# The order of rounded and remainder rows in the second block of each feed-forward pair

## The reference, cut to what matters

```
def swiglu(x, w_gate, w_up, w_down):
    return (jax.nn.silu(x @ w_gate) * (x @ w_up)) @ w_down

h = x
for i in range(DEPTH):                       # DEPTH = 2
    h = h + 0.5 * swiglu(rms_norm(h, norm_ff1[i]), ffn1_gate[i], ffn1_up[i], ffn1_down[i])
    hn = rms_norm(h, norm_mix[i])
    h = h + (hybrid mixer of hn if i is even, differential attention of hn if i is odd)
    h = h + 0.5 * swiglu(rms_norm(h, norm_ff2[i]), ffn2_gate[i], ffn2_up[i], ffn2_down[i])
return rms_norm(h, final_norm)
```

## Time and profile before

| | |
|---|---|
| median of 3 runs | 1066.17 us |
| the profiled execution's own time | 1065.55 us |
| its span in the profile | 1063.7 us |
| PE busy | 1050.4 us (99%), 6678 matmuls |
| PEld busy | 944.8 us (89%) |
| DVE busy | 792.3 us (74%) |
| ACT busy | 611.4 us (57%) |
| DMA queue of the weights | 188.89 MB, 63.0% of 16 engines |

### The profile page before, as it was taken

How to read it: one execution, slowest core, us unless ns; L and a number is a source line. 1 busy time by engine, 2 the same in 40 slices (tenths; PEclk the granted TensorE clock), 3 DMA queues, 4 the chain that set the end, 5 groups by cost and what they waited for, 6 DMA issues and landing times.

```text
span 1063.7 us, 18486 instructions
## 1 busy us (share of the span) xinstructions
PE 1050.4 (99%) x6678; PEld 944.8 (89%) x6678; DVE 792.3 (74%) x1137; ACT 611.4 (57%) x980; POOL 51.1 (5%) x70
## 2 busy tenths in 40 slices
PE   9999999999999999999999999999999999999997
PEld 8888888899998998888888888888999998888886
DVE  6788776679868878887666888776699578888653
ACT  6555554468976665555445665543456756656541
POOL 0200011100000000000111000011100000000011
PEclk9999999999998999999999999999999999999999
DMA  8866775549644656667755666685566446667671
GB/s 250 213 195 193 211 205 162 156 124 259 175 114 125 200 156 191 189 194 206 208 158 159 196 196 189 197 218 165 146 169 165 120 127 200 190 195 204 188 200 40
DMA packets 369283, 190.14 MB, mean 179 GB/s; under 512 B 5920, under 2 KB 368704, under 8 KB 369232
## 3 DMA queue, kind: packets, MB, share of 16 engines
q1 hardware_dynamic: 368976, 188.89, 63.0%
q0 software_dynamic: 256, 0.59, 0.3%
HBM read 187.86 MB, written 1.07 MB: 178 GB/s over the span
## 4 chain that ended last, share of the span: by engine, by line
PE 94%; ACT 3%; DVE 2%; issue 1%; DVEq 0%; ACTq 0%
PE psum L217 45%; PE psum L220 24%; PE psum L201 7%; PE psum L205 7%; PE psum L202 6%; PE psum L1898 1%; ACT whi L185 1%; PE psum L1523 1%; DVE wlo L190 1%; PE psum L966 0%; DVE arena L1195 0%; PE psum L956 0%; PE psum L883 0%; PE psum L939 0%; PE psum L957 0%
## 5 line engine op out<-in xcount | busy, mean ns | idle before, releaser
L190 DVE TENSOR_TENSOR wlo<-raw,whi 128x1024 fp32r<-128x1024 f32 (+1 forms) x324 | 416.9, 1305 | 76.1 <-ACT whi L185 74.7
L185 ACT ACTIVATE whi<-raw 128x1024 fp32r<-128x1024 f32 (+1 forms) x324 | 354.0, 1113 | 35.0 <-PE psum L205 26.3
L217 PE MATMUL psum<-xn,whi 128*128 128x512 f32 x1408 | 354.3, 393 | 0.5 <-DVE xn L307 0.5
L217 PEld LDWEIGHTS psum<-xn,whi 128*128 128x128 f32 x1408 | 253.4, 189 | 46.7 <-issue 0.6
L220 PEld LDWEIGHTS psum<-xn,wlo 128*128 128x128 f32 x1408 | 192.4, 190 | 13.8
L220 PE MATMUL psum<-xn,wlo 128*128 128x256 f32 x1408 | 196.9, 282 | 0.0
L217 PE MATMUL psum<-hid,whi 128*128 128x512 f32 x704 | 171.8, 391 | 0.0
L217 PEld LDWEIGHTS psum<-hid,whi 128*128 128x128 f32 x704 | 128.1, 189 | 24.0
L201 PE MATMUL psum<-xn,whi 128*128 128x256 f32 x480 | 122.1, 292 | 0.9 <-ACT whi L185 0.9
L202 PE MATMUL psum<-xn,whi 128*128 128x256 f32 x480 | 118.9, 285 | 0.0
L510 ACT ACTIVATE arena<-arena 128x256 f32<-128x256 f32 x88 | 36.8, 419 | 112.4 <-DVE arena L574 112.4
(11 more groups left out here) (230 smaller groups left out, 873.1 us busy)
## 6 DMA issues: line engine op xcount, KB each, us to landing
raw<-in_ffn_gate SPq DMA_DIRECT2D x88, 512.0 KB, 3.9
raw<-in_ffn_up SPq DMA_DIRECT2D x88, 512.0 KB, 3.9
raw<-in_ffn_down SPq DMA_DIRECT2D x64, 704.0 KB, 4.6
raw<-in_hyb_w_in SPq DMA_DIRECT2D x36, 512.0 KB, 4.9
raw<-in_dif_w_qkv SPq DMA_DIRECT2D x24, 512.0 KB, 4.5
raw<-in_hyb_w_out SPq DMA_DIRECT2D x16, 512.0 KB, 4.7
raw<-in_dif_w_o SPq DMA_DIRECT2D x8, 512.0 KB, 4.1
hid<-cs_rows SPq DMA_DIRECT2D x4, 512.0 KB, 6.9
```

Source lines behind the costliest of these rows:

```text
L185: act.activation(whi[:, s, 0:k * P], raw[:, s, 0:k * P], ACT.Copy).then_inc(s_whi, 1)
L190: dve.tensor_tensor(wlo[:, s, 0:k * P], raw[:, s, 0:k * P], whi[:, s, 0:k * P].bitcast(F32), ALU.subtract).then_inc(s_wlo, 1)
L217: pe.matmul(acc, hi[:, j, :], x[:, t, :, :], start=start and j == 0, stop=False)
```

## The change

`multiply_wide` gets a flag `lo_first`, which is set for the second block of each pair (m == 1), in the gate/up part and in the down part. With it the block waits for `s_wlo` at its start. In the gate/up part, where the second block opens a PSUM bank of its own, one wide matmul comes first, since it has to set both halves of the bank; then come the 8 narrow ones and then the other 7 wide ones. In the down part, where the bank is open already, all 11 narrow ones come first and then all 11 wide ones. Where `need` is given, it is now called before narrow matmuls too. The number of matmuls, their operands and the other engines' instructions stay as they are.

```
-        def multiply_wide(pe, b, s, k, x, k0, acc, start=True, stop=True, need=None, part=None):
+        def multiply_wide(pe, b, s, k, x, k0, acc, start=True, stop=True, need=None, part=None, lo_first=False):
             hi, lo = tile_of(whi, s, k), tile_of(wlo, s, k)
-            pe.wait_ge(s_whi, b + 1)
-            for j in part or range(k):
-                t = k0 + j
-                if need:
-                    need(t)
-                pe.matmul(acc, hi[:, j, :], x[:, t, :, :], start=start and j == 0, stop=False)
-            pe.wait_ge(s_wlo, b + 1)
-            for j in part or range(k):
-                mm = pe.matmul(acc[:, T:2 * T], lo[:, j, :], x[:, k0 + j, 0, :], start=False,
-                               stop=stop and j == k - 1)
-            if j == k - 1:
+            def rounded(tiles, first, last):
+                mm = None
+                for j in tiles:
+                    if need:
+                        need(k0 + j)
+                    mm = pe.matmul(acc, hi[:, j, :], x[:, k0 + j, :, :], start=first and j == 0, stop=last and j == k - 1)
+                return mm
+            def remainders(tiles, first, last):
+                mm = None
+                for j in tiles:
+                    if need:
+                        need(k0 + j)
+                    mm = pe.matmul(acc[:, T:2 * T], lo[:, j, :], x[:, k0 + j, 0, :], start=first and j == 0,
+                                   stop=last and j == k - 1)
+                return mm
+            tiles = part or range(k)
+            if lo_first:
+                pe.wait_ge(s_wlo, b + 1)
+                begin = 1 if start else 0
+                rounded(tiles[:begin], start, False)
+                remainders(tiles, False, False)
+                mm = rounded(tiles[begin:], False, stop)
+            else:
+                pe.wait_ge(s_whi, b + 1)
+                rounded(tiles, start, False)
+                pe.wait_ge(s_wlo, b + 1)
+                mm = remainders(tiles, False, stop)
+            if not part or k - 1 in part:
                 mm.then_inc(s_blk, 1)
...
-                                      part=part)
+                                      part=part, lo_first=m == 1)
...
-                                  need=need)
+                                  need=need, lo_first=m == 1)
```

## The result

The changed kernel took 1070.79 us (median of 13 runs, 1068.73 to 1073.26) against 1066.32 for the kernel before (13 runs, 1064.57 to 1068.67): 4.5 us more by the medians. The recorded ratio of the two is 1.0033 with a 95% interval of 1.0025 to 1.0041, which is 2.7 to 4.4 us more. So it is slower. The prediction was 1070.4, in a range of 1067.8 to 1073.6. The span of the profiled execution grew from 1063.7 to 1069.0 us.

A forecast was written before the change was run, and what follows sets the result against it. PE, busy 99% of the span, was taken as the bound. Stalls of 2.0 + 3.4 + 1.2 = 6.6 us less 2.2 gave 4.4 more: 1069.95 from the profiled time, 1070.6 from the median, stated as 1070.4, range 1067.8 to 1073.6.

The forecast's parts named there:

- Part one: Gate/up and down pairs: joining runs of one kind quickens PE's matmuls, 1.8 us plus 0.5 us gained, entered as 2.2.
- The heads: Start of each run after a change of kind: a wide run loses 0.025 us, a narrow run gains 0.01.
- the lone wide matmul: Gate/up pairs: the single wide matmul opening the second bank between narrow runs, priced at 0.23 us against 0.227, 0.003 extra.
- the rival at 1072.2: All pairs: the pace doesn't change, so 6.6 us more, 1072.2 from the profiled time; chance 0.12.
- Part two: Second block of a stage's first gate/up pair: remainder row asked for 1.84 us earlier, late in three stages, 2.01 us.
- the restart: At each of seven stalls: PE starting again costs 0.18 us beyond the operand's lateness, 1.2 us in all.
- The 0.2 us for feed-forward 0: Start of feed-forward 0, gate/up: remainder row 0.03 us late, counted as a stall with 0.18 us for starting again.
- The rival of a supply that slips in the first loop of feed-forward 0: Second gate/up pair there: remainder rows come late if DMA or ACT lags, 1 to 2 us on top; chance 0.08.
- Part three: First down pair of each stage, second block: narrow matmuls ask for hidden tile 21 too early, 4 x 0.84 = 3.4 us.
- No later wait swallows it: After the stalls: later PE waits are for ACT and DVE work begun at PE blocks, so the 4.4 us stays.
- The sum: Whole kernel: 2.0 + 3.4 + 1.2 = 6.6 us of stalls, less 2.2 of pace, 4.4 us more.
- seven: Stalls expected: three at the starts of feed-forward 0, 2 and 3, four at hidden tile 21 in the down parts.

The follow-up runs named there:

- Experiment 7: experiment 3 with its gate/up pairs' lone wide matmul moved into the first block's wide run (9 wide, 16 narrow, 7 wide): 1063.24 us against 1067.26 before, ratio 0.9967.
- experiment 3: The kernel before with the new order in all pairs but each stage's first gate/up and first down pair: 1063.89 us against 1067.09, ratio 0.9980.
- experiment 2: The kernel before with the new order in the down pairs alone, gate/up pairs unchanged: 1069.87 us, ratio 1.0024.
- experiment 4: The changed kernel, but first-down-pair narrow matmuls wait only for the rounded half of their hidden tile: 1070.2 us, ratio 1.0029 to the kernel before.
- experiment 5: experiment 2 with 2, 0, 4, 4 wide matmuls (feed-forward 0 to 3) ahead of the narrow ones in the first down pair's second block: 1068.78 us, one run.
- experiment 1: The kernel before with the new order in the gate/up pairs alone, down pairs unchanged: 1067.21 us against 1067.09, ratio 1.0007.

## Why the prediction was right

**Part one, the pace: right in kind, too large in gate/up.** The heads are there and one of each goes where runs join. I had 0.02 us for a gate/up pair, 1.8 us in all. Where nothing stalls, the gate/up parts are shorter by 0.28 and 0.22 us with 22 pairs each, so 0.011 a pair and 1.0 us in all. The term that was mis-sized is the price of the lone wide matmul. A wide head is worth 0.027 us by the single starts, a little more than my 0.025. But the lone wide matmul costs 0.007 where I had 0.003, the 8 narrow ones behind it take 0.958 us instead of 0.953, and the 15 wide ones that follow take 0.002 us more than 15 with an ordinary head. The trace of before had such a one, but with one narrow matmul behind it, not 8. Experiment 7 removes it and has 0.39 us a part, close to the 21 x 0.020 = 0.42 that one wide head less the gain of one narrow head gives in 21 pairs. The down part had 0.015 us a pair and 0.5 in all; a pair gives 0.020, as my heads came from rows of two decimals, and the part 0.6 in all (experiment 3: 0.58 for 28 pairs). The rule of the page "TensorE: Matmul & The Clock Gate" in the Trainium skill ("Back-to-back issue gap"), by which part one is worth nothing, belonged to the rival at 1072.2. The section gives its formula for an isolated matmul at the full clock, with the number of columns alone in it; here 512 columns take 0.227 to 0.242 us in the device loops, by what ran before them, and experiments 3 and 7, at 0.2 and 0.3% below the kernel before with the same matmuls in another order, exclude it for this kernel.

**Part two, the remainder row: right in two stages of three.** Taking the length of the parts and adding back the pace, feed-forward 2 has 1.36 us with the restart where I had 1.12 + 0.18, feed-forward 3 has 1.07 where I had 0.86 + 0.18; by the starts it is 1.33 and 1.07. Feed-forward 1 has none, as forecast. The 0.2 us for feed-forward 0 did not come; an operand late by 0.03 us was inside what one execution differs from another (the first block started 10.62 us into the span before, 10.96 after, and up to 11.7 in the experiments). That a row late by so little was counted as a full stall was the weak step of this part. The rival of a supply that slips in the first loop of feed-forward 0 did not come either: the list has no entry for it, and that part is shorter than before by 0.28 us.

**Part three, the hidden tile: right in place, cause and size.** Four stalls of 1.03 us by the starts, where I had 0.84 + 0.18. Measured it is 0.88 of lateness and 0.16 for the restart. The forecast left out that the joined wide run saves the down part its first head, so that PE asks 0.03 us sooner; in experiment 2, without that, the lateness is 0.84, as forecast. Experiments 4 and 5 show that it is this tile: an earlier operand and a later request each shorten the stall by just as much as they should.

**No later wait swallows it: right.** The mixers behind the stalls are as long as before (0.02 us), so each stall reaches the end in full.

**The sum.** Forecast 6.6 - 2.2 = 4.4 us. Measured in the parts: 4.89, which is 4 x 1.03 + 1.36 + 1.07 = 6.55 of stalls, less 1.66 of pace (what is left between the two). The forecast's gain was 0.5 us too large, and its stalls right to 0.1 with one of seven missing and the others a little dearer. That the median of 1070.79 lies 0.4 us from the 1070.4 is in part luck, as the runs of this kernel go from 1068.73 to 1073.26; the terms, measured one by one in the parts, bear the forecast out.

## What to carry to other kernels

Where one engine is the bound at 99%, reordering its instructions is not free even if it adds none: list for each moved instruction when it now asks for its operand, and compare that with the end of the writer, first of all in the first pairs of a stage, where the writers have no lead yet. A cheap run that is moved ahead of a dear one brings every request behind it forward by the difference of the two. Make such an edit in the steady loop alone: here 112 of 120 pairs gave 1.6 us, and the other 8 took 6.5.

## What the runs showed of the hardware that was not expected

**The pace of fp32r matmuls.** At the full granted clock a wide matmul (512 columns) takes 0.227 us from start to start in a long run, and a narrow one (256 columns) 0.120, more than half of it. After narrow ones the wide ones take 0.233, 0.236, 0.228, 0.233 and 0.231 before they settle, in 228 of the 240 blocks of the kernel before; the other 12 are at the starts of the stages. What causes this ramp was not tried. When the kinds alternate, it becomes a cycle of three tiles.

**Why runs of one kernel scatter by 2 to 4 us.** The times go with the mean granted clock of the run. Among the 43 runs of the kernel before beside the experiments, those at 0.997 took 1064.3 to 1064.6 us, those at 0.995 1064.5 to 1065.9, and those at 0.992 1068.0 to 1068.9. The profiles show where the clock differs most. The mixer behind feed-forward 0 has a stretch at half clock (1.2 GHz): from 323 to 329 us of the kernel before the granted clock is 0.50. Its length differs between the profiled executions, though no kernel here changes a mixer. Rows of 28 us, 322 to 350 us, of the kernel before, of experiment 1 and of experiment 3 (stretch: its length, busy us and count of PE, PEld, DVE, ACT and POOL, granted clock, DMA share, GB/s):

```profile
322.00:350.00 28.00, 26.69 (x191) 26.13 (x192) 23.42 (x38) 17.36 (x25) 0.00 (x0) 0.88 0.51 147
```
```profile
322.00:350.00 28.00, 26.70 (x182) 26.21 (x182) 23.49 (x38) 16.89 (x25) 0.00 (x0) 0.82 0.51 147
```
```profile
322.00:350.00 28.00, 26.69 (x168) 26.20 (x168) 21.86 (x35) 15.51 (x24) 0.00 (x0) 0.76 0.46 130
```

PE is equally busy in all three, but gets through 191, 182 and 168 matmuls. The mixer is longer than in the profile of before by 1.23 us in experiment 1 and 2.86 us in experiment 3, while the mixer of experiment 7, at a mean of 0.88 again, differs by 0.01. The profiled execution of experiment 3 took 1068.32 us though the median of its runs is 1063.89. Against the profile of before it has 2.86 us in that mixer, 1.10 by a later start of the first block and 0.4 at its end, less the 1.6 of the edit. This is why the lengths of the parts, and not the spans, carry the verdicts above. What sets the length of the stretch stays open; experiments 2 and 5, which differ in a few matmuls alone, have a mixer that is 0.05 us shorter and one that is 1.19 us longer, so I see no tie to the edit, but no experiment was made on it.
